# A hybrid decoder layer on one core: LRU gates as pairs of 64-row products, elementwise work of the tile reordered, GLA gates in three row groups

## The reference, cut to what matters

```python
xb = xc.reshape(b_, l_, LRU_BLOCKS, LRU_BLOCK)            # 16 blocks of 64 channels
r = sigmoid(einsum('blki,kij->blkj', xb, wa) + ba)        # block-diagonal products
i = sigmoid(einsum('blki,kij->blkj', xb, wx) + bx)
log_a = -LRU_C * r * softplus(-lam)
a = exp(log_a)
u = sqrt(-expm1(2.0 * log_a)) * (i * xc)                  # expm1 gives 1 - a*a
h = scan(a, u)                                            # h = a * h_before + u
y = h * gelu(gate_in)
b_lru = y @ W['w_lru_out']
...
g_log = log_sigmoid(g_low @ W['gla_w_alpha'] + W['gla_b_alpha']) / GLA_TAU   # rank 16
```

## Time and profile before

| | |
|---|---|
| median of 3 runs | 2849.0 us (2847.8 to 2850.08) |
| profiled execution | 2849.57 us |
| its span in the profile | 2847.4 us |
| PE busy | 2788.5 us, 98% |
| DVE, ACT, POOL busy | 1431.3, 742.1, 1075.5 us |
| PE's share of the chain that ended last | 86% |

### The profile page before, as it was taken

How to read it: one execution, slowest core, us unless ns; L and a number is a source line. 1 busy time by engine, 2 the same in 40 slices (tenths; PEclk the granted TensorE clock), 3 DMA queues, 4 the chain that set the end, 5 groups by cost and what they waited for, 6 DMA issues and landing times.

```text
span 2847.4 us, 43317 instructions
## 1 busy us (share of the span) xinstructions
PE 2788.5 (98%) x18106; PEld 2633.0 (92%) x18106; DVE 1431.3 (50%) x2023; ACT 742.1 (26%) x1421; POOL 1075.5 (38%) x729
## 2 busy tenths in 40 slices
PE   7999999999999999999999999999999999999999
PEld 7999999897979799999777999998989999999998
DVE  7987002332232326722875310425368776677664
ACT  4555001221222211223983211214231000001002
POOL 4332222221212223323452444311258888873221
PEclk9999999999999999999999999999999999999999
DMA  4111222121221352224445433244222222225222
GB/s 127 38 38 39 71 68 61 48 73 50 58 68 40 102 189 84 77 66 127 154 140 149 146 106 98 61 152 136 77 69 68 84 82 63 84 81 205 93 91 78
DMA packets 319568, 259.15 MB, mean 91 GB/s; under 512 B 32906, under 2 KB 290123, under 8 KB 319376
## 3 DMA queue, kind: packets, MB, share of 16 engines
q1 hardware_dynamic: 230976, 153.38, 18.5%
q10 hardware_dynamic: 88400, 103.01, 10.9%
HBM read 198.84 MB, written 57.51 MB: 90 GB/s over the span
## 4 chain that ended last, share of the span: by engine, by line
PE 86%; DVE 7%; ACT 4%; issue 2%; ACTq 1%; DMA 0%; POOL 0%; SPq 0%; DVEq 0%; POOLq 0%
PE PS L977 39%; PE PS L1683 16%; PE PS L1699 8%; PE PS L1011 5%; PE PS L1067 4%; DVE WK L2641 3%; PE PS L1053 2%; PE PS L1075 1%; PE PS L1561 1%; PE PS L1537 1%; PE PS L1090 1%; PE PS L1715 1%; PE PM L1233 1%; PE PS L1253 1%; PE PS L1258 1%
## 5 line engine op out<-in xcount | busy, mean ns | idle before, releaser
L887 POOL CAST Wh<-Wr 128x1024 fp32r<-128x1024 f32 x169 | 193.1, 1143 | 1514.5 <-DMA Wr<-in_w_in 797.7
L977 PE MATMUL PS<-Hh,Wh 128*128 128x384 f32 (+1 forms) x1928 | 636.5, 330 | 7.5 <-POOL Wl L889 2.0
L977 PE MATMUL PS<-Hh,Wl 128*128 128x384 f32 (+1 forms) x1928 | 630.0, 327 | 0.0
L977 PE MATMUL PS<-Hl,Wh 128*128 128x384 f32 (+1 forms) x1928 | 629.5, 326 | 0.0
L889 POOL TENSOR_TENSOR Wl<-Wr,Wh 128x1024 fp32r<-128x1024 f32 x169 | 435.2, 2575 | 13.5
L977 PEld LDWEIGHTS PS<-Hh,Wh 128*128 128x128 f32 x1928 | 362.8, 188 | 11.5 <-issue 6.4
L977 PEld LDWEIGHTS PS<-Hl,Wh 128*128 128x128 f32 x1928 | 362.9, 188 | 0.9 <-issue 0.2
L977 PEld LDWEIGHTS PS<-Hh,Wl 128*128 128x128 f32 x1928 | 362.6, 188 | 0.0
L2641 DVE SCALAR_TENSOR_TENSOR WK<-WK,PS 128x384 f32<-128x384 f32 (+1 forms) x120 | 63.1, 532 | 437.9 <-PE PS L977 269.1
L3258 DVE TENSOR_TENSOR X<-X,PS 128x384 f32<-128x384 f32 (+1 forms) x264 | 136.9, 531 | 125.6 <-PE PS L1699 79.5
L977 PE MATMUL PS<-Yh,Wh 128*128 128x384 f32 (+1 forms) x576 | 188.1, 327 | 1.5 <-DVE Yl L2951 1.5
(11 more groups left out here) (512 smaller groups left out, 5543.9 us busy)
## 6 DMA issues: line engine op xcount, KB each, us to landing
Wr<-in_w_in SPq DMA_DIRECT2D x82, 512.0 KB, 3.9
X<-f_scr SPq DMA_DIRECT2D x11, 1088.0 KB, 5.1
Wr<-in_w_ffn_gate SPq DMA_DIRECT2D x22, 512.0 KB, 3.8
Wr<-in_w_ffn_up SPq DMA_DIRECT2D x22, 512.0 KB, 4.4
Wr<-in_w_ffn_down SPq DMA_DIRECT2D x22, 512.0 KB, 3.7
merged<-WK ACTq DMA_DIRECT2D x16, 544.0 KB, 3.6
WK<-gates ACTq DMA_DIRECT2D x16, 544.0 KB, 4.8
WK<-merged ACTq DMA_DIRECT2D x16, 544.0 KB, 6.1
```

Of the source, the lines that this page charges most:

```text
L887: pool.tensor_copy(Wh[:, n % SLOTS], Wr[:, n % SLOTS]).then_inc(w_hi, 1)
L977: mm = pe.matmul(bank(f"{name}:{g}")[:, 0:n], L[:, w % SLOTS, k, :], R[:, k, t0:t0 + n], start=(k == 0 and i == 0), stop=(last and k == DT ...
```

## The change

The gate products of a tile become pairs. A weight tile now holds, for the first head, `wa` beside `wx` and, for the second, `wx` beside `wa`. One product contracts 64 rows of one head and gives r and i together; the two of a pair use different halves of PE's rows and different banks (group 0 goes to `PM`, groups 1 and 2 to four banks of the ring). Their readers work on 64 partitions at a time, so each tanh of a column group is two instructions. Gelu's polynomial becomes one DVE instruction (its factor goes into ACT's square), the squared decay moves from DVE to ACT, and `Yh` and `Yl` of a tile move into the next tile; the copies that signal `cb` move behind `y`. The low-rank gate is computed three times over in rows 0, 32 and 64 (the weight tile is loaded as four transfers of 32 columns), and the three products of `ga{h}` use three groups of rows. `gla_w_alpha` is loaded three times, `lru_bx` in two swapped halves. Some semaphores are shared.

```diff
-             for _name, _banks in (("ga", (1, 2, 4)), ("gq", (0, 3, 5)), ("gk", (1, 2, 4)))}
+             for _name, _banks in (("ga", (1, 2, 4)), ("gq", (3, 5, 0)), ("gk", (4, 1, 2) if _h == 2 else (1, 2, 4)))}
...
-        banks(f"lr{t}")
-        banks(f"li{t}")
+        for g in (1, 2):
+            jobs.extend([f"la{t}:{g}", f"lb{t}:{g}"])
...
+                halves = wk(0)[R_BX:R_BX + 1, 0:D].rearrange("r (t two j) -> r t two j", two=2, j=64)
+                for h in range(2):
+                    sp.dma_start(halves[:, :, 1 - h], I["lru_bx"].rearrange("r (t two j) -> r t two j", two=2, j=64)[:, :, h])\
+                        .then_inc(packs, 16)
...
-                        sp.dma_start(YA[64 * h:64 * h + 64, DT:2 * DT, i * P + 64 * h:i * P + 64 * h + 64],
+                        col = 64 * (i if h == 0 else 1 - i)
+                        sp.dma_start(YA[64 * h:64 * h + 64, DT:2 * DT, col:col + 64],
...
-                    for i, start in enumerate((C_LOW, C_DT)):
-                        tile = I["w_in"][0, :, start:start + 64]
-                        ins = sp.dma_start(Wr[:, n % SLOTS, :, 64 * i:64 * i + 64], tile.rearrange("(k p) m -> p k m", p=P))
-                        ins.then_inc(w_loaded[n % SLOTS] if i else S("dt_in"), 16)
+                    for i, start in enumerate((C_LOW, C_LOW, C_LOW, C_DT)):
+                        tile = I["w_in"][0, :, start:start + 32]
+                        ins = sp.dma_start(Wr[:, n % SLOTS, :, 32 * i:32 * i + 32], tile.rearrange("(k p) m -> p k m", p=P))
+                        ins.then_inc(w_loaded[n % SLOTS] if i == 3 else S("dt_in"), 16)
...
-            def fp32_all(name, lhsT, rhs):
-
+            def head_gates(t):
+
+                if t:
+                    pe.wait_ge(S("l0_free"), t)
                 for g, (t0, n) in enumerate(GROUPS):
-                    free_bank(pe, f"{name}:{g}")
-                    done(pe.matmul(bank(f"{name}:{g}")[:, 0:n], lhsT, rhs[:, t0:t0 + n], start=True, stop=True),
-                         f"{name}:{g}")
+                    for h in range(2):
+                        rows = slice(64 * h, 64 * h + 64)
+                        if g:
+                            name = f"l{'ab'[h]}{t}:{g}"
+                            free_bank(pe, name)
+                        out = bank(name) if g else PM[:, h]
+                        mm = pe.matmul(out[:, 0:n], YA[rows, DT + t, 0:P], XC(t)[rows, t0:t0 + n], start=True, stop=True)
+                        if g:
+                            done(mm, name)
+                        else:
+                            mm.then_inc(S("l0"), 1)
...
+                for g, (t0, n) in enumerate(GROUPS):
+                    rows = slice(32 * g, 32 * g + 16)
+                    free_bank(pe, f"ga{h}:{g}")
+                    done(pe.matmul(bank(f"ga{h}:{g}")[:, 0:n], CB[rows].rearrange("p k c -> p (k c)")[:, h % 2 * P:h % 2 * P + P],
+                                   wk(3)[rows, t0:t0 + n], start=True, stop=True), f"ga{h}:{g}")
...
-                act.activation(wk(6)[:, 0:T], GB(t), ACT.Square).then_inc(S("g_sq"), 1)
+                act.activation(wk(6)[:, 0:T], GB(t), ACT.Square, scale=0.044715 ** 0.5).then_inc(S("g_sq"), 1)
                 if t + 1 < DT:
                     copy_lx(t + 1)
                 else:
                     all_groups("og0_0", wk(1), ACT.Tanh, scale=0.5)
+                if t:
+                    act.activation(Yh[:, t - 1], GB(t - 1), ACT.Copy).then_inc(S("y_hi"), 1)
                 if t == 0:
                     act.wait_ge(S("dve_step"), STEP["sc"])
-                all_groups(f"lr{t}", wk(2), ACT.Tanh, bias=SC[:, t, 1:2], scale=0.5)
+                for g, (t0, n) in enumerate(GROUPS):
+                    for h in range(2):
+                        rows = slice(64 * h, 64 * h + 64)
+                        if g:
+                            ready(act, f"l{'ab'[h]}{t}:{g}")
+                        else:
+                            act.wait_ge(S("l0"), 2 * t + h + 1)
+                        src = bank(f"l{'ab'[h]}{t}:{g}") if g else PM[:, h]
+                        ins = act.activation(wk(2)[rows, t0:t0 + n], src[rows, 0:n], ACT.Tanh, bias=SC[rows, t, 1:2],
+                                             scale=0.5)
+                link(ins)
                 link(act.activation(wk(3)[:, 0:T], wk(2)[:, 0:T], ACT.Tanh, bias=SC[:, t, 0:1], scale=SC[:, t, 0:1]))
-                act.activation(wk(2)[:, 0:T], wk(2)[:, 0:T], ACT.Exp, bias=NSC[:, t:t + 1],
-                               scale=NSC[:, t:t + 1]).then_inc(S("a"), 1)
-                all_groups(f"li{t}", wk(4), ACT.Tanh, bias=SC[:, t, 2:3], scale=0.5)
+                link(act.activation(wk(2)[:, 0:T], wk(2)[:, 0:T], ACT.Exp, bias=NSC[:, t:t + 1], scale=NSC[:, t:t + 1]))
+                if t:
+                    act.wait_ge(S("cb"), t)
+                act.activation(wk(7)[:, 0:T], wk(2)[:, 0:T], ACT.Square).then_inc(S("a"), 1)
+                for g in (1, 2, 0):
+                    t0, n = GROUPS[g]
+                    for h in range(2):
+                        rows, other = slice(64 * h, 64 * h + 64), slice(64 - 64 * h, 128 - 64 * h)
+                        src = bank(f"l{'ab'[h]}{t}:{g}") if g else PM[:, h]
+                        ins = act.activation(wk(4)[rows, t0:t0 + n], src[other, 0:n], ACT.Tanh, bias=SC[other, t, 2:3],
+                                             scale=0.5)
+                        if g:
+                            freed(ins, f"l{'ab'[h]}{t}:{g}")
+                ins.then_inc(S("l0_free"), 1)
                 act.wait_ge(S("g_inner"), t + 1)
                 act.activation(wk(6)[:, 0:T], wk(6)[:, 0:T], ACT.Tanh, scale=GELU_C).then_inc(S("g_tanh"), 1)
                 act.wait_ge(S("u_var"), t + 1)
@@ -1948,16 +1991,16 @@
                         act.wait_ge(S("y_lo"), t)
                     all_groups(f"lg{t + 1}", GB(t + 1), ACT.Copy)
                 act.wait_ge(S("y"), t + 1)
-                act.activation(Yh[:, t], GB(t), ACT.Copy).then_inc(S("y_hi"), 1)
+            act.activation(Yh[:, DT - 1], GB(DT - 1), ACT.Copy).then_inc(S("y_hi"), 1)
...
-                act.dma_start(CB[0:16].rearrange("p k c -> p (k c)")[:, h % 2 * P:h % 2 * P + P],
-                              I["gla_w_alpha"][0, :, h * P:(h + 1) * P]).then_inc(S(f"wal{h % 2}"), 16)
+                for i in range(3):
+                    act.dma_start(CB[32 * i:32 * i + 16].rearrange("p k c -> p (k c)")[:, h % 2 * P:h % 2 * P + P],
+                                  I["gla_w_alpha"][0, :, h * P:(h + 1) * P]).then_inc(S(f"wal{h % 2}"), 16)
...
+            def y_low(t):
+
+                dve.wait_ge(S("y"), t + 1)
+                dve.wait_ge(S("y_hi"), t + 1)
+                dve.tensor_tensor(Yl[:, t], GB(t), Yh[:, t].bitcast(F32), SUB).then_inc(S("y_lo"), 1)
             for t in range(DT):
                 G = GB(t)
                 dve.wait_ge(S("g_sq"), t + 1)
-                link(dve.tensor_scalar(GP, GP, 0.044715, 1.0, MUL, ADD))
-                dve.tensor_tensor(GP, GP, G, MUL).then_inc(S("g_inner"), 1)
+                stt(GP, GP, 1.0, G, ADD, MUL).then_inc(S("g_inner"), 1)
                 if t + 1 < DT:
                     conv_lx(t + 1)
+                if t:
+                    y_low(t - 1)
 
                 dve.wait_ge(S("a"), t + 1)
-                link(dve.tensor_tensor(U, A, A, MUL))
                 stt(TZ, U, 1.0, TZ, ADD, MUL).then_inc(S("u_var"), 1)
-                for g in range(3):
-                    read(dve, f"li{t}:{g}")
+                dve.wait_ge(S("l0_free"), t + 1)
                 link(stt(TI, TI, 1.0, XC(t), ADD, MUL))
                 dve.wait_ge(S("u_mult"), t + 1)
                 link(dve.tensor_tensor(TI, TI, TZ, MUL))
@@ -2802,15 +2851,12 @@
                 link(dve.tensor_tensor(seqs(TI)[:, :, 0], seqs(TI)[:, :, 0], LAM[:, 0], ADD))
                 link(dve.memset(seqs(A)[:, :, 0:1], 0.0))
                 link(dve.tensor_tensor_scan(U, A, TI, 0.0, MUL, ADD))
-                dve.tensor_copy(CB[:, t, 27:28], U[:, LP - 1:LP])
-                dve.tensor_copy(CB[:, t, 28:36], seqs(U)[:, :, LS - 1]).then_inc(S("cb"), 1)
                 dve.wait_ge(S("g_tanh"), t + 1)
                 link(stt(GP, GP, 1.0, G, ADD, MUL))
                 stt(G, GP, 0.5, U, MUL, MUL).then_inc(S("y"), 1)
-                dve.wait_ge(S("y"), t + 1)
-                dve.wait_ge(S("y_hi"), t + 1)
-                ins = dve.tensor_tensor(Yl[:, t], G, Yh[:, t].bitcast(F32), SUB)
-                ins.then_inc(S("y_lo"), 1)
+                dve.tensor_copy(CB[:, t, 27:28], U[:, LP - 1:LP])
+                dve.tensor_copy(CB[:, t, 28:36], seqs(U)[:, :, LS - 1]).then_inc(S("cb"), 1)
+            y_low(DT - 1)
```

38 lines of the change are left out of this document (19 added, 19 removed).

## The result

The changed kernel takes 2869.8 us (median of 4 runs, 2865.0 to 2873.9), the kernel before 2849.5 (median of 4): a ratio of 1.0069, 95% interval 1.0056 to 1.0083. It is 20 us slower where 4.9 were forecast. Its profiled execution took 2864.96 us, the fastest of the four, with a span of 2862.7 against 2847.4 before: 15.3 us more.

What follows compares the result with a forecast made beforehand. PE bounded the LRU before, the loop through ACT and DVE with POOL's delays after. LRU and its tail +9.6, GLA -6.4, the rest +1.65 make +4.85 us; 2849.0 + 4.9 = 2853.9 us, range 2841 to 2860.

Steps and rivals of the forecast that it cites:

- PE's side: LRU gates on PE: pairs run together, 2.2 us instead of 3.66, so PE alone needs 25.9 us a tile.
- The loop through ACT and DVE: LRU, from one `y` to the next: ACT 17.7 us, DVE 6.95, with handoffs 24.8, below PE's 25.9.
- six half tanhs 2.95: ACT's first set of half tanhs in an LRU tile: 2.95 us, if half the partitions cost what all do.
- six more tanhs 2.7: ACT's second set of half tanhs in an LRU tile, behind the moved square: 2.7 us.
- POOL and the scan: LRU loop: POOL's instructions hold up DVE's scan and the next product, adding 2.65 us a tile.
- main case: The forecast itself, with POOL costing 2.65 us a tile: 2853.9 us, own range 2850 to 2858, chance 0.48.
- the first rival: LRU: the scan is not held up by POOL, the loop stays under 25.9 us: 2842.4 us, chance 0.22.
- The second rival: LRU: POOL falls whole on the loop, 3.4 us for 2.65, 28.2 a tile: 2858.4 us, chance 0.20.
- The sum of both: LRU loop with POOL's cost: 24.8 + 2.65 = 27.45 us a tile in five tiles.
- Behind the last tile: PE after the last LRU gates: waits 12.2 us for `cb`, 40.5 us instead of 30.5, plus 1.8 for the clock.
- GLA: GLA gates in three row groups take 0.84 us a head and `gq:0` needn't wait: -6.4 us over four heads.
- The rest: Waits moved by the bank ring, +0.6 and +0.7 us, and one more small SP transfer, +0.35: +1.65 us.

Runs made afterwards that it cites:

- e_lru_loop: Changed kernel with half tanhs ordered by halves, squared decay back on DVE and POOL's second split behind `y`: 2850.0 us in one run.
- e_head_major: Changed kernel with each set of six half tanhs ordered by halves, rows 0 to 63 first, then 64 to 127: 2857.1 us in one run.
- e_pool_hold: Changed kernel with POOL's second split of each LRU tile held until that tile's `y` is written: 2854.0 us in one run.
- e_gq_bank: Changed kernel with `gq`'s banks 5, 3, 0 instead of 3, 5, 0 in heads 1 to 3: 2866.8 us in one run.
- e_lru_only: Kernel before with the LRU part of the change alone, GLA's gates, loads and banks as before: 2875.4 us, ratio 1.0091.
- e_best: Changed kernel with `e_lru_loop`'s edits, CB copies ahead of `y`, `og0_1` projected ahead of CB's transposes, `gq` banks 5, 3, 0, later `lru_bx`: 2833.5 us.
- e_cb_first: Changed kernel with the two copies to CB right behind the scan, ahead of the products that make `y`: 2872.1 us in one run.
- the best kernel: `e_best` with ACT's tanhs of `og0_1` ahead of its copies of CB's transposes and `gk` banks 4, 1, 2 in head 1 too: 2827.6 us.
- e_best2_free: The best kernel without the two lines that hold POOL's splits back: 2839.4 us in one run.

## Why the prediction was wrong

The prediction was wrong in size, on the side of its forecast: 2853.9 us forecast, 2869.8 measured, beyond the 2860 of its range. The mechanism it named for the LRU is the one that was found.

- *PE's side.* Right. Pairs start together, PE alone needs 25.92 us a tile (25.9 forecast), as `e_lru_loop` shows.
- *The loop through ACT and DVE.* Here is the step that failed, and it is a term of the sum: "six half tanhs 2.95" and "six more tanhs 2.7". They take 3.45 and 3.50, 1.3 us more per tile. The text had said that no row shows whether a half tanh costs what a full one does, and then took the row's value with no bound on the other side. `e_head_major` shows that the cost isn't the half but the change of partitions from one tanh to the next: within a half, starts are 0.48 us apart. Without POOL the loop was put at 24.8 us; `e_pool_hold` measures 26.35. Of the 1.55 between them 1.3 are the tanhs; the other 0.25 has no term.
- *POOL and the scan.* Right, in the main case's size: 2.65 us forecast; 0.72 ahead of the scan and 1.94 in it in the trace of the kernel after, 2.37 of a tile's spacing in `e_pool_hold`. The scan is held up where POOL's instruction starts ahead of it, in tiles 1 to 5, so the first rival falls; in tile 7, where the scan starts first, it does keep its 2.42 us beside POOL, which the prediction had named as a sign against itself. The second rival has a time nearer to the result, but not for its reason: POOL cost less than it says, not more.
- *The sum of both.* 27.45 and 1.3 for the tanhs are 28.7, the measured spacing. Six tiles of 1.2 to 1.4 us are the 7.7 us by which the stretch from first to last gates missed.
- *Behind the last tile.* Right within 1.3 us: 12.2 us forecast for the wait, 11.59 measured; +11.8 in all, +13.1 measured. That the wait fits so well is partly luck: `cb` is done 29.7 us after the last gates start (27.8 forecast), and `low` only 18.1 us after (15.6 forecast). The last gates take 4.45 us instead of 2.2, since they wait 1.62 us for a bank that ACT's tanh of `og0_0` frees, and a short drop of the clock follows them, besides the one behind the wait.
- *GLA.* The gates take the 0.84 us forecast once nothing waits (0.85 in `e_gq_bank`), but "`gq:0` in bank 3 needn't wait" was wrong: it waits 1.05 to 1.17 us for DVE's reciprocal, which lies behind the last products of a head, 3.4 us in three heads. That leaves 2.4 of the 5.8 us summed; 1.8 are measured, and the other 0.6 was not followed. The GLA part by itself is worth about 6 by the medians; what hides it in the comparison is, as far as one trace of `e_lru_only` shows, that GLA as it was before is slower behind the changed LRU.
- *The rest.* The two halves of `lru_bx` take 1.51 us to issue, not two of 0.28; each gathers pieces of 64 columns, but that this is the reason wasn't tried. PE is 1.2 us later instead of 0.35; a later place for them gives 0.7 back (`e_best`), and the rest wasn't followed. The wait at `ob2_0` came as forecast.

Of the 10.5 us between forecast and the profiled execution (+4.85 and +15.3), 7.7 are the tanhs, 4.0 GLA, 1.3 the tail, 0.85 the start, and SSD gave 3.4 back. The median lies another 4.9 over the profiled execution. Which stage holds that wasn't seen, as only one execution of the changed kernel has a trace. SSD's offset moves by -5.3 to +8.9 us between 1320 and 1545 us in kernels that are alike there, which makes it the likely place, no more: `e_cb_first` and `e_pool_hold` also lose 4.1 and 5.2 us between 2400 and 2800 us.

## What to carry to other kernels

An edit that shortens the engine which sets the pace is worth only the distance to the next loop; work out that loop with every moved instruction in it, and give each term that no row shows a bound on both sides, above all when it is taken several times a turn. Then ask which other engine delays instructions in the loop's exposed part: here two lines that let POOL start later took 2.37 us off a tile, more than any other single edit to the loop, and still 8.0 us off the best kernel's first stage. The pairs pay off without them too, but less (`e_best2_free`, 2839.4 us in one run, against 2827.6). Last, when a rotation of buffers turns by other numbers, go through the first wait of each later stage again.
